# Gated linear mixer with five small experts: keys' level factors on VectorE, the norm's gains folded into the copies of the turned rows

## The chip, the cores and the metric

The kernel runs on 1 core of one Trainium2 chip. The metric is the device time of the whole program in microseconds (us), lower is better. Before the change the median of 3 runs is 1949.45 us (1948.65, 1949.45 and 1952.14).

## The reference

256 tokens of width 1024 go through a first block (three attention branches with gates and a feed-forward) and then a second block of two layers. The change lies in the mixer of the second block's first layer, a gated linear recurrence of 8 heads of width 128:

- from the rows h: forget gates f (a sigmoid, scaled between a lower bound and 1), queries q (silu), values v, output gates g (a sigmoid), keys k = 1 - f;
- for each head a running sum c of log f over the tokens; the output of token t is the sum over s up to t of (q_t exp(c_t - c_s) k_s) v_s;
- the output of each head is divided by its root mean square, multiplied by the vector `hg_norm_g_2` (128 gains, the same for each head) and by the gate g, and multiplied by `hg_w_out_2`.

Behind it follow a layer norm, a feed-forward of width 2816, a second layer with differential attention, and 8 experts of width 3584 for the chosen tokens.

## The kernel before

The program is written by hand for each engine, with semaphores. Every weight is read from HBM into a ring of three 2 MB slots (SP's queue, `load`), cut into pieces, and each piece is split into a high part (ScalarE, L1255) and a low part (VectorE, L1862); each product of rows and weights is then three matmuls (TensorE, L437 to L439). A slot is loaded again as soon as VectorE has split its last piece. VectorE's and ScalarE's programs are sequences in a fixed order: `pieces_done` and `piece_done` stand between the other work and take one piece each.

**The mixer's stage** (some 480 to 640 us of the profile). The recurrence is not run over tokens but in levels. For a block size b of 128, 64, 32, 16, 8, 4, 2, 1 (`LEVELS`, levels 0 to 7) tokens are taken in pairs of blocks; a query in the second block of a pair meets a key in the first, and the decay between them is split at the block's border into a factor of the query and one of the key. Level 8 is the diagonal, without factors. For each level:

- `level_differences` (VectorE, L2243; L2240 for level 0): the sums c minus c at the border, 128x2048;
- `level_exps` (ScalarE, L1540 and L1541): the two exponentials, 128x1024 each, the keys' and the queries';
- `level_queries` (VectorE, L2253): queries times factor into QS, 128x1024;
- `level_keys` (GpSimd, L2844): keys times factor into KS, 128x1024, with the other operands in the same form;
- `level` (TensorE, L885): 32 matmuls of 128x128 in fp32 (16 for level 0) of KS and QS into four PSUM banks; it waits for both factors;
- `level_place` (VectorE, L2263, levels 2 and up): four masked copies from PSUM into STT. Levels 0 and 1 are copied by ScalarE (`level_copy`, L1552, L1554).

The levels stand between the projections for g and v: TensorE does two pieces of a projection (24 matmuls of 512 columns) and then one level (`LEVEL_AT`). VectorE does two splits, the next level's differences, this level's four copies, the next level's queries. QS and KS exist once, so the queries and keys of a level wait for the matmuls of the level before (`T["level", i - 1]`).

The gate rows (GN, in the buffer BC) get tanh on ScalarE (L1561), times 0.5 plus 0.5 on VectorE (`gate_rows2`, L2270), and the norm's gains on GpSimd (`gain_gates`, L2852, four 128x512, with NG[:, 0] as a row spread over the partitions). GpSimd does `gain_gates("hg0")` behind level 3 and `gain_gates("hg1")` behind level 5. GpSimd also sets RM, STT, KS and QS and computes KK ahead of the levels (L2828 to L2835).

At the end VectorE multiplies the outputs by the root (L2312) and by GN (L2315), TensorE turns them (`columns("ho")`, L457), ScalarE copies the turned rows to XH (`column_halves`, L1273) and VectorE computes XL from PSUM and XH (`column_lows`, L1890), as operands for the product with `hg_w_out_2`. In the turned rows a partition is one of the 128 columns of a head. The vectors that are needed this way stand in VS, one row each, loaded by small DMAs of SP's queue at the start (`VECTORS`, L2943), turned once by TensorE into VT.

Of the kernel before, what the change touches and what calls it, by code (L numbers as in the profile page):

```python
# [53 lines left out]

V_MIX, V_MEM, V_FFN, V_LNG, V_LNB, V_QF, V_KF, V_QC, V_KC, V_LB = 0, 8, 16, 24, 56, 88, 89, 90, 91, 92

# [66 lines left out]
def build(nc, I, table, out):  # L123
    ctx = ExitStack()
    with ctx:
# [17 lines left out]
        BC = sb("BC", [128, 2, D])  # L143
        NG = sb("NG", [128, 2, 128])
        GM = sb("GM", [128, 2, 64])
# [63 lines left out]
        s_ed, s_ee, s_qs, s_ks, s_lv, s_stt, s_vv = (sem(n) for n in ("s_ed", "s_ee", "s_qs", "s_ks", "s_lv", "s_stt", "s_vv"))  # L209
        s_gth, s_gg, s_ggp, s_osq, s_od = (sem(n) for n in ("s_gth", "s_gg", "s_ggp", "s_osq", "s_od"))  # L210
        s_lam, s_lme, s_rx, s_ru, s_mix, s_dsq, s_doo = (sem(n) for n in ("s_lam", "s_lme", "s_rx", "s_ru", "s_mix", "s_dsq", "s_doo"))
# [125 lines left out]
        PM, PMT = ar(AR1, 2048, 2, 512), ar(AR1, 3072, 2, 512)  # L337
        VECTORS = [(V_FFN, "g_ffn", 8), (V_LNG, "ln_g_2", 32), (V_LNB, "ln_b_2", 32), (V_LB, "hg_lb_2", 24), (V_QC, "g_q_mem", 1), (V_KC, "g_k_mem", 1)]
        ONE = AR1[:, 17408:17536]
# [79 lines left out]
        def pe_program(e):  # L419
# [261 lines left out]
            room(7)  # L681
            pe.wait_ge(s_vec, 16 * 10)
            e.transpose(PS[7][:, 0:128], VS[:, 0:128], ident).then_inc(banks.put("vt", 7), 1)
# [553 lines left out]
        def act_program(e):  # L1237
# [25 lines left out]

            def column_halves(name, scale=None, tts=(0, 1), halves=(0, 1)):
                for tt in tts:
                    a.wait_ge(*T["xfree", name, tt])
                    for half in halves:
                        j = 2 * tt + half
                        a.wait_ge(*banks.full["cols", name, j])
                        ps = PS[banks_of[name][j]].rearrange("p (a n) -> p a n", a=4)  # L1270
                        x = XH[:, 4 * half:4 * half + 4, 128 * tt:128 * tt + 128]
                        if scale is None:
                            e.activation(x, ps, ACT.Copy).then_inc(s_colh, 1)  # L1273
                        else:
                            a.wait_ge(*banks.out["vt0" if scale == V_MEM else "vt"])
                            for k in range(4):
                                c = scale + 4 * half + k
                                t = e.activation(x[:, k, :], ps[:, k, :], ACT.Copy, scale=VT[:, c:c + 1])
                            t.then_inc(s_colh, 1)
# [311 lines left out]
            for tt in range(2):  # L1591
                for g in range(2):
# [3 lines left out]
                    e.activation(SQ2[:, tt, 512 * g:512 * g + 512], PS[2 * tt + g][:, :], ACT.Square).then_inc(s_osq, 1)  # L1596
            column_halves("ho")

# [252 lines left out]
        def dve_program(e):  # L1851
# [28 lines left out]

            def column_lows(name, scale=None, tts=(0, 1), halves=(0, 1)):
                for tt in tts:
                    for half in halves:
                        j = 2 * tt + half
                        v.wait_ge(s_colh, col_at(name, tt, half))
                        ps = PS[banks_of[name][j]].rearrange("p (a n) -> p a n", a=4)
                        xs = (slice(None), slice(4 * half, 4 * half + 4), slice(128 * tt, 128 * tt + 128))
                        h2, l2 = XH[xs], XL[xs]
                        if scale is None:
                            e.tensor_tensor(l2, ps, h2.bitcast(F32), ALU.subtract).then_inc(s_cols, 1)  # L1890
                        else:
                            for k in range(4):
                                c = scale + 4 * half + k
                                t = e.scalar_tensor_tensor(out=l2[:, k, :], in0=ps[:, k, :], scalar=VT[:, c:c + 1], in1=h2[:, k, :].bitcast(F32), op0=ALU.mult, op1=ALU.subtract)
                            t.then_inc(s_cols, 1)
# [26 lines left out]
            def unit_rows(n):  # L1922
                nh = HEADS[n]
                for tt in range(2):
# [10 lines left out]
                    if n in GAIN_ROW:  # L1935
                        v.wait_ge(s_bc, 16 * 8)
                        v.wait_ge(*banks.out["p", n, tt])
                        e.tensor_tensor(x, x, GM[:, GAIN_ROW[n], :].unsqueeze(1).to_broadcast([128, 8, 64]), ALU.mult).then_inc(s_gn, 1)
# [41 lines left out]
            def forget(stage):  # L1980
                if stage == 0:
                    v.wait_ge(*banks.full["fg", 0])
                    e.tensor_copy(NCT[0:8], PS[3][0:8, 0:256]).then_inc(banks.out["fg", 0][0], 1)
                    v.wait_ge(*banks.full["fg", 1])
                    v.wait_ge(s_bc, 16 * 8)
                    e.tensor_tensor(FZ, PS[3][:, 256:272].rearrange("p (a h) -> p a h", a=2), BFG[:, :].unsqueeze(1).to_broadcast([128, 2, 8]), ALU.add).then_inc(banks.out["fg", 1][0], 1)
# [78 lines left out]
            first_layer(ITEMS[2:4])  # L2065
            v.wait_ge(s_bc, 16 * 8)
            for i, w in enumerate((WFG, WRT)):
# [177 lines left out]
            def level_queries(i):  # L2245
# [7 lines left out]
                e.tensor_tensor(qsv[:, :, 1, :], qv[:, :, 1, :], ev[:, :, 1, :], ALU.mult).then_inc(s_qs, 1)  # L2253

            def level_place(i):

                for n in range(2):
                    for g in range(2):
                        b = 4 + (2 * n + g + 2) % 4
                        v.wait_ge(*banks.full["lv", i, n, g])  # L2260
                        v.wait_ge(s_set, 2)
                        m = LEVM[:, 128 * (i - 1):128 * i].unsqueeze(1).to_broadcast([128, 4, 128])
                        e.copy_predicated(STT[:, n, 4 * g:4 * g + 4, :], m, PS[b][:, :].rearrange("p (j n) -> p j n", j=4)).then_inc(banks.out["lv", i, n, g][0], 1)  # L2263
# [20 lines left out]
            pieces_done(4)  # L2284
            level_queries(0)
            for n in ("hg0", "hg1", "hv0", "hv1"):
                for q in range(4):
# [3 lines left out]
                    if (n, q) in LEVEL_AT:  # L2291
# [5 lines left out]
                        if i + 1 < 8:  # L2297
                            level_queries(i + 1)
            level_place(8)
            for tt in range(2):  # L2300
# [4 lines left out]
            v.wait_ge(s_ee, 8)  # L2305
            v.wait_ge(s_ggp, 4)
            for tt in range(2):
                for g in range(2):
# [6 lines left out]
                    e.tensor_tensor(ov, ov, GN[:, tt, 512 * g:512 * g + 512], ALU.mult).then_inc(s_od, 1)  # L2315
            column_lows("ho")
            norm_between(0, ("ho0", "ho1"), ((0, 1), (6, 7)), "F2")
# [22 lines left out]
            t_nl = v.step(e.tensor_scalar(NL, NL, -LAM_INIT, None, ALU.add))  # L2340
            t_ng = v.step(e.tensor_scalar(NG[:, 1, :], NG[:, 1, :], 1.0 - LAM_INIT, None, ALU.mult))

# [35 lines left out]
            def da_rows(g):  # L2378
                r = root(("da", g))
                for q in range(2):  # L2380
# [4 lines left out]
                    v.wait_ge(*t_ng)  # L2385
                    e.tensor_tensor(ov, ov, NG[:, 1, :].unsqueeze(1).to_broadcast([128, 4, 128]), ALU.mult).then_inc(s_doo, 1)

# [350 lines left out]
        def pool_program(e):  # L2738
# [44 lines left out]
            for tt in range(2):  # L2783
                inverse_root(("kc", tt))
            for dst, name, n in ((GM[:, 0, :], "g_q_moba", 64), (GM[:, 1, :], "g_k_moba", 64), (NG[:, 0, :], "hg_norm_g_2", 128),
                                 (NG[:, 1, :], "da_norm_g_2", 128), (LAMB[:, :], "da_lam_2", 256), (BFG[:, :], "b_forget", 8)):
                e.dma_start(dst, spread(I[name], n)).then_inc(s_bc, 16)
# [42 lines left out]
            e.memset(STT, 0.0).then_inc(s_set, 1)  # L2830
            t_ks = p.step(e.memset(KS, 0.0))
            p.wait_ge(s_sg, 8)
            e.tensor_scalar(KK, SG, -1.0, 1.0, ALU.mult, ALU.add).then_inc(s_kk, 1)
            p.wait_ge(*T["scan"])
            e.memset(QS, 0.0).then_inc(s_q0, 1)  # L2835
            p.wait_ge(*t_ks)
            p.wait_ge(s_kk, 1)

            def level_keys(i):
                ev, kv, ksv = (flat(x).rearrange("p (y x b) -> p y x b", x=2, b=LEVELS[i]) for x in (EE, KK, KS))  # L2840
                p.wait_ge(s_ee, i + 1)
                if i:
                    p.wait_ge(*T["level", i - 1])
                e.tensor_tensor(ksv[:, :, 0, :], kv[:, :, 0, :], ev[:, :, 0, :], ALU.mult).then_inc(s_ks, 1)  # L2844

            def gain_gates(n):
                c = int(n[2])
                p.wait_ge(s_bc, 16 * 8)
                for tt in range(2):
                    g4 = GN[:, tt, 512 * c:512 * c + 512].rearrange("p (h d) -> p h d", h=4)  # L2850
                    p.wait_ge(s_gg, 2 * c + tt + 1)
                    e.tensor_tensor(g4, g4, NG[:, 0, :].unsqueeze(1).to_broadcast([128, 4, 128]), ALU.mult).then_inc(s_ggp, 1)  # L2852

            level_keys(0)
            for i in range(1, 8):
                level_keys(i)
                if i == 3:
                    gain_gates("hg0")
                if i == 5:
                    gain_gates("hg1")  # L2860
            for tt in range(2):
# [259 lines left out]
```

## Time and profile before

| | us |
|---|---|
| median of 3 runs | 1949.45 |
| the profiled execution | 1949.79 |
| its span, first to last instruction | 1948.0 |
| TensorE busy | 1846.0 (95%) |
| VectorE busy | 1487.8 (76%) |
| ScalarE busy | 1219.4 (63%) |
| GpSimd busy | 166.6 (9%) |

The granted clock of TensorE is 0.98 of full over the span. The busy shares are means over stages with different limits. For this change only the stage with the levels counts, and there the duration of a single VectorE instruction beside GpSimd's, and the starts of the level's matmuls, say more than a share.

### The profile page before, as it was taken

The numbers are of one execution on the slowest core, as the hardware profiler recorded it, in microseconds if no ns is written. First come the engines' busy times: TensorE is split into PE (matmuls) and PEld (weight loads), VectorE is DVE, ScalarE is ACT, GpSimd is POOL, SyncE is SP. The second block draws the span as 40 slices with busy tenths as digits, with TensorE's granted clock in tenths as the row PEclk, the third lists the DMA queues.
The fourth block names the chain that finished last, engine by engine and source line by source line (L and its number), as shares of the span: only waits on it lengthen the run. The fifth ranks groups of instructions, "written<-read, shape, count | busy, mean of one in ns | idle before, by whom it ended". The sixth has DMA issues, their size and how long they took to land.

```text
span 1948.0 us, 22339 instructions
## 1 busy us (share of the span) xinstructions
PE 1846.0 (95%) x9128; PEld 1527.8 (78%) x9128; DVE 1487.8 (76%) x1424; ACT 1219.4 (63%) x1267; POOL 166.6 (9%) x128
## 2 busy tenths in 40 slices
PE   7999999999998899988979999999999999999997
PEld 6888878888987688877757887877888787788875
DVE  5645566444689754467678989999988999998897
ACT  6555546343653444335536778888777888877784
POOL 2501100000233310023120000000000000000000
PEclk9999999999999999989988999999999999999999
DMA  8434445445432465435246999999999999999994
GB/s 290 172 130 136 151 175 187 174 172 195 146 114 87 152 229 182 151 136 181 95 175 224 379 353 399 409 413 409 404 370 365 400 409 413 409 405 371 358 410 177
DMA packets 154813, 511.61 MB, mean 263 GB/s; under 512 B 4447, under 2 KB 8913, under 8 KB 140369
## 3 DMA queue, kind: packets, MB, share of 16 engines
q1 hardware_dynamic: 152672, 504.53, 68.3%
q0 software_dynamic: 1424, 4.59, 0.8%
q8 instruction: 74, 1.21, 0.3%
q10 hardware_dynamic: 608, 0.99, 0.1%
q14 instruction: 35, 0.28, 0.0%
HBM read 509.05 MB, written 1.05 MB: 262 GB/s over the span
## 4 chain that ended last, share of the span: by engine, by line
PE 68%; DVE 18%; DMA 7%; ACT 4%; issue 2%; POOL 0%; ACTq 0%; SPq 0%; DVEq 0%; POOLq 0%
PE PS L437 19%; PE PS L439 18%; PE PS L438 18%; DVE WLB L1862 6%; DMA ring<-in_moe_w_down 6%; DVE WLX L1862 5%; PE PS L1104 1%; PE PS L1105 1%; ACT WHX L1255 1%; ACT WHB L1255 1%; PE PS L885 1%; PE PS L1035 1%; PE PS L1037 1%; DVE AR L2253 1%; PE PS L582 1%
## 5 line engine op out<-in xcount | busy, mean ns | idle before, releaser
L1862 DVE TENSOR_TENSOR WLB<-ring,WHB 128x2048 fp32r<-128x2048 f32 (+1 forms) x344 | 645.9, 1894 | 118.6 <-ACT WHB L1255 118.1
L1255 ACT ACTIVATE WHB<-ring 128x2048 fp32r<-128x2048 f32 (+1 forms) x344 | 532.6, 1561 | 317.9 <-PE PS L439 283.9
L1862 DVE TENSOR_TENSOR WLX<-ring,WHX 128x2048 fp32r<-128x2048 f32 (+1 forms) x216 | 469.0, 2192 | 54.2 <-ACT WHX L1255 54.0
L1255 ACT ACTIVATE WHX<-ring 128x2048 fp32r<-128x2048 f32 (+1 forms) x216 | 393.4, 1838 | 160.1 <-PE PS L439 124.3
L437 PE MATMUL PS<-WHB,XH 128*128 128x512 f32 (+1 forms) x640 | 259.2, 405 | 14.8 <-DVE XL L1911 6.8
L439 PE MATMUL PS<-WHB,XL 128*128 128x512 f32 (+1 forms) x640 | 251.2, 392 | 0.0
L438 PE MATMUL PS<-WLB,XH 128*128 128x512 f32 (+1 forms) x640 | 250.8, 392 | 0.0
L437 PEld LDWEIGHTS PS<-WHB,XH 128*128 128x128 f32 x640 | 123.0, 192 | 43.5 <-issue 11.7
L2743 POOL TENSOR_TENSOR SM<-SM,MH 128x8 f32<-128x8 f32 (+3 forms) x28 | 38.2, 1368 | 1352.8 <-DVE SM L1875 1352.8
L439 PEld LDWEIGHTS PS<-WHB,XL 128*128 128x128 f32 x640 | 122.6, 192 | 26.5
L438 PEld LDWEIGHTS PS<-WLB,XH 128*128 128x128 f32 x640 | 123.1, 192 | 23.4
L1058 PE MATMUL PS<-WHB,EH 128*128 128x512 f32 x280 | 113.0, 404 | 4.2 <-DVE WLB L1862 3.3
L1058 PE MATMUL PS<-WHX,EH 128*128 128x512 f32 x280 | 113.7, 406 | 3.5 <-DVE WLX L1862 2.5
L1059 PE MATMUL PS<-WLX,EH 128*128 128x512 f32 x280 | 109.6, 391 | 0.0
L1059 PE MATMUL PS<-WLB,EH 128*128 128x512 f32 x280 | 109.5, 391 | 0.0
L437 PE MATMUL PS<-WHX,XH 128*128 128x512 f32 (+1 forms) x240 | 92.2, 384 | 4.7 <-DVE WLX L1862 4.7
L439 PE MATMUL PS<-WHX,XL 128*128 128x512 f32 (+1 forms) x240 | 91.0, 379 | 0.0
L438 PE MATMUL PS<-WLX,XH 128*128 128x512 f32 (+1 forms) x240 | 90.8, 378 | 0.0
L437 PE MATMUL PS<-WHB,HTH 128*128 128x512 f32 x184 | 72.3, 393 | 0.0
L439 PE MATMUL PS<-WHB,HTL 128*128 128x512 f32 x184 | 71.7, 390 | 0.0
L438 PE MATMUL PS<-WLB,HTH 128*128 128x512 f32 x184 | 71.6, 389 | 0.0
L1058 PEld LDWEIGHTS PS<-WHB,EH 128*128 128x128 f32 x280 | 52.6, 188 | 22.5 <-DVE WLB L1862 12.3
(416 smaller groups left out, 3441.4 us busy)
## 6 DMA issues: line engine op xcount, KB each, us to landing
ring<-in_moe_w_gate SPq DMA_DIRECT2D x56, 2048.0 KB, 11.0
ring<-in_moe_w_up SPq DMA_DIRECT2D x56, 2048.0 KB, 11.3
ring<-in_moe_w_down SPq DMA_DIRECT2D x56, 2048.0 KB, 11.8
ring<-in_w_in SPq DMA_DIRECT2D x13, 2048.0 KB, 8.1
ring<-in_hg_w_in SPq DMA_DIRECT2D x8, 2048.0 KB, 8.5
ring<-in_da_w_in SPq DMA_DIRECT2D x6, 2048.0 KB, 8.0
ring<-in_w_gate SPq DMA_DIRECT2D x5, 2048.0 KB, 7.8
ring<-in_w_up SPq DMA_DIRECT2D x5, 2048.0 KB, 7.8
```

The source lines that it names most:

```text
L437: e.matmul(o, xh, wh, start=start, stop=False)
L438: e.matmul(o, xh, wl, start=False, stop=False)
L439: return e.matmul(o, xl, wh, start=False, stop=stop)
L582: t = e.matmul(PS[4 + q][:, dv * h:dv * h + dv], PTBUF[a][h % 2][:, 128 * j:128 * j + 128], VR[VK[a]][:, k, dv * h:dv * h + dv], start=(k ...
L885: t = e.matmul(PS[b][:, 128 * j:128 * j + 128], a_k[:, h, 128 * s_t:128 * s_t + 128], a_q[:, h, 128 * t_t:128 * t_t + 128], start=True, st ...
L1035: t = e.matmul(PS[b][:, at_:at_ + 64], src[:, tt, 128 * d:128 * d + 128], PO[:, tt, 0:64], start=(tt == 0), stop=(tt == 1))
L1037: t = e.matmul(PS[b][:, 128 * j:128 * j + CAP], src[:, tt, 128 * d:128 * d + 128], PO[:, tt, :], start=(tt == 0), stop=(tt == 1))
L1058: e.matmul(PS[b][:, :], EH[:, kt, :], wh, start=(kt == 0), stop=False)
L1059: t = e.matmul(PS[b][:, :], EH[:, kt, :], wl, start=False, stop=(kt == 7))
L1255: e.activation(hi, src, ACT.Copy).then_inc(s_hi, 1)
L1862: e.tensor_tensor(lo, src, hi.bitcast(F32), ALU.subtract).then_inc(s_lo, 1)
L2743: e.tensor_tensor(RR[name], RV[name], MH[:, 0:RR[name].shape[1]], ALU.pow).then_inc(s_rs, 1)
```

## The change

`level_keys` moves from GpSimd's program to VectorE's, behind `level_queries` of the same level. `gain_gates` goes away; the gains come in as a per-partition scale in ScalarE's copy of the turned rows and in VectorE's low part of them. For this `hg_norm_g_2` is loaded by SP's queue as row 116 of VS (a DMA more) instead of being spread into NG by GpSimd's queue (a DMA less), and NG is half as large. VectorE waits for s_gg where it waited for s_ggp.

```diff
-V_MIX, ..., V_LB = 0, 8, 16, 24, 56, 88, 89, 90, 91, 92
+V_MIX, ..., V_LB, V_HN = 0, 8, 16, 24, 56, 88, 89, 90, 91, 92, 116
-        NG = sb("NG", [128, 2, 128])
+        NG = sb("NG", [128, 128])
-        VECTORS = [..., (V_LB, "hg_lb_2", 24), (V_QC, "g_q_mem", 1), ...]
+        VECTORS = [..., (V_LB, "hg_lb_2", 24), (V_HN, "hg_norm_g_2", 1), (V_QC, "g_q_mem", 1), ...]
-            pe.wait_ge(s_vec, 16 * 10)
+            pe.wait_ge(s_vec, 16 * 11)
 # ScalarE, column_halves(..., one=None)
+                        if one is not None:
+                            e.activation(x, ps, ACT.Copy, scale=VT[:, one:one + 1]).then_inc(s_colh, 1)
-            column_halves("ho")
+            column_halves("ho", one=V_HN)
 # VectorE, column_lows(..., one=None)
+                        if one is not None:
+                            e.scalar_tensor_tensor(out=l2, in0=ps, scalar=VT[:, one:one + 1], in1=h2.bitcast(F32), op0=ALU.mult, op1=ALU.subtract).then_inc(s_cols, 1)
-                        v.wait_ge(s_bc, 16 * 8)
+                        v.wait_ge(s_bc, 16 * 7)
 # VectorE
+            def level_keys(i):
+                ev, kv, ksv = (flat(x).rearrange("p (y x b) -> p y x b", x=2, b=LEVELS[i]) for x in (EE, KK, KS))
+                v.wait_ge(s_ee, i + 1)
+                v.wait_ge(s_set, 3)
+                v.wait_ge(s_kk, 1)
+                if i:
+                    v.wait_ge(*T["level", i - 1])
+                e.tensor_tensor(ksv[:, :, 0, :], kv[:, :, 0, :], ev[:, :, 0, :], ALU.mult).then_inc(s_ks, 1)
             level_queries(0)
+            level_keys(0)
...
                             level_queries(i + 1)
+                            level_keys(i + 1)
-            v.wait_ge(s_ggp, 4)
+            v.wait_ge(s_gg, 4)
-            column_lows("ho")
+            column_lows("ho", one=V_HN)
 # GpSimd
-            t_ks = p.step(e.memset(KS, 0.0))
+            e.memset(KS, 0.0).then_inc(s_set, 1)
...
-            def level_keys(i): ...
-            def gain_gates(n):
-                c = int(n[2])
-                p.wait_ge(s_bc, 16 * 8)
-                for tt in range(2):
-                    g4 = GN[:, tt, 512 * c:512 * c + 512].rearrange("p (h d) -> p h d", h=4)
-                    p.wait_ge(s_gg, 2 * c + tt + 1)
-                    e.tensor_tensor(g4, g4, NG[:, 0, :].unsqueeze(1).to_broadcast([128, 4, 128]), ALU.mult).then_inc(s_ggp, 1)
-            level_keys(0)
-            for i in range(1, 8):
-                level_keys(i)
-                if i == 3:
-                    gain_gates("hg0")
-                if i == 5:
-                    gain_gates("hg1")
```

## Rows read from the trace of the kernel before

**Rows 1.** The page, part 2: the DMA engines' busy tenths in 40 slices of the span

```profile
DMA  8434445445432465435246999999999999999994
```

**Rows 2.** The chain that ended last, inside the levels (start us, us, what)

```profile
579.99 2.20 DVE AR L2243
582.19 2.54 DVE AR L2263 x4
...
587.74 1.13 DVE WLB L1862
588.87 0.67 DVE BC L2270 x2
```

**Rows 3.** Windows from level to level: length, busy PE, PEld, DVE, ACT, POOL; clock; DMA

```profile
575.60:587.80 12.20, 9.36 (x57) 8.02 (x57) 12.20 (x9) 4.17 (x5) 5.65 (x3) 1.00 0.00 0
587.80:598.60 10.80, 10.80 (x56) 9.69 (x57) 10.80 (x11) 3.69 (x4) 3.58 (x2) 0.84 0.55 196
```

**Rows 4.** Timeline of VectorE (DVE) in the levels

```profile
561.41 1.23 DVE L2253 TENSOR_TENSOR AR<-AR 128x1024 f32<-128x1024 f32 x1 [3.46 <-ACT AR L1541]
562.55 3.41 DVE L1862 TENSOR_TENSOR WLB<-ring,WHB 128x1024 fp32r<-128x1024 f32 x1
...
572.40 3.17 DVE L2253 TENSOR_TENSOR AR<-AR 128x1024 f32<-128x1024 f32 x1
575.49 4.50 DVE L1862 TENSOR_TENSOR WLB<-ring,WHB 128x1024 fp32r<-128x1024 f32 x2
...
618.15 3.84 DVE L2253 TENSOR_TENSOR AR<-AR 128x1024 f32<-128x1024 f32 x1
```

**Rows 5.** Timeline of GpSimd (POOL) in the levels

```profile
561.45 3.42 POOL L2844 TENSOR_TENSOR AR<-AR 128x1024 f32<-128x1024 f32 x1 [7.93 <-ACT AR L1541]
572.09 2.40 POOL L2844 TENSOR_TENSOR AR<-AR 128x1024 f32<-128x1024 f32 x1 [7.22 <-ACT AR L1541]
574.45 4.46 POOL L2852 TENSOR_TENSOR BC<-BC,NG 128x512 f32<-128x512 f32 x2
...
618.03 2.88 POOL L2844 TENSOR_TENSOR AR<-AR 128x1024 f32<-128x1024 f32 x1 [7.85 <-ACT AR L1541]
```

**Rows 6.** TensorE's level matmuls: timeline for levels 1 to 4, chain for 7, 8

```profile
553.62 5.44 PE L885 MATMUL PS<-AR 128*128 128x128 f32 x32 [2.02 <-issue]
564.98 3.81 PE L885 MATMUL PS<-AR 128*128 128x128 f32 x32 [0.40 <-issue]
575.62 3.84 PE L885 MATMUL PS<-AR 128*128 128x128 f32 x32 [1.33 <-DVE AR L2253]
587.79 5.46 PE L885 MATMUL PS<-AR 128*128 128x128 f32 x32 [2.82 <-DVE AR L2253]
...
622.31 7.15 PE PS L885 x64
```

**Rows 7.** Timeline of ScalarE: the exponentials of levels 1 and 2

```profile
549.01 1.04 ACT L1541 ACTIVATE AR<-AR 128x1024 f32<-128x1024 f32 x1
...
559.38 1.05 ACT L1540 ACTIVATE AR<-AR 128x1024 f32<-128x1024 f32 x1
```

**Rows 8.** Single lines: copies and subtractions with and without a pointer scale (min/median/max ns)

```profile
L1353 ACT ACTIVATE AR<-PS,VT x4: 669/674/681, 33.5 to 68.0; 128x512 f32<-128x512 f32 x4
...
L1273 ACT ACTIVATE XH<-PS x16: 592/597/600, 275.8 to 990.8; 128x512 fp32r<-128x512 f32 x16
...
L1932 DVE SCALAR_TENSOR_TENSOR AR<-PS,SM x2: 739/740/741, 30.1 to 30.8; 128x512 f32<-128x512 f32 x2
...
L1890 DVE TENSOR_TENSOR XL<-PS,XH x16: 681/684/692, 277.9 to 991.5; 128x512 fp32r<-128x512 f32 x16
```

**Rows 9.** Timeline of the start: a small DMA of SP's queue, ScalarE's third split

```profile
6.77 0.25 SPq L2944 DMA_DIRECT2D VS<-in_g_k_mem  x1
...
23.64 1.06 ACT L1255 ACTIVATE WHB<-ring 128x1024 fp32r<-128x1024 f32 x1 [0.42 <-PE PS L439]
```

**Rows 10.** Waits of SP's queue over the span: total us, times, longest

```profile
SPq L2933 <- DVE WLB L1862: 1154.4, 132, 32.8
```

More of the change, by code:

```diff
@@ L53 @@
 C_END = 2112
-V_MIX, V_MEM, V_FFN, V_LNG, V_LNB, V_QF, V_KF, V_QC, V_KC, V_LB = 0, 8, 16, 24, 56, 88, 89, 90, 91, 92
+V_MIX, V_MEM, V_FFN, V_LNG, V_LNB, V_QF, V_KF, V_QC, V_KC, V_LB, V_HN = 0, 8, 16, 24, 56, 88, 89, 90, 91, 92, 116
 def constant_table():
@@ L209, in build @@
         s_ed, s_ee, s_qs, s_ks, s_lv, s_stt, s_vv = (sem(n) for n in ("s_ed", "s_ee", "s_qs", "s_ks", "s_lv", "s_stt", "s_vv"))
-        s_gth, s_gg, s_ggp, s_osq, s_od = (sem(n) for n in ("s_gth", "s_gg", "s_ggp", "s_osq", "s_od"))
+        s_gth, s_gg, s_osq, s_od = (sem(n) for n in ("s_gth", "s_gg", "s_osq", "s_od"))
         s_lam, s_lme, s_rx, s_ru, s_mix, s_dsq, s_doo = (sem(n) for n in ("s_lam", "s_lme", "s_rx", "s_ru", "s_mix", "s_dsq", "s_doo"))
@@ L337, in build @@
         PM, PMT = ar(AR1, 2048, 2, 512), ar(AR1, 3072, 2, 512)
-        VECTORS = [(V_FFN, "g_ffn", 8), (V_LNG, "ln_g_2", 32), (V_LNB, "ln_b_2", 32), (V_LB, "hg_lb_2", 24), (V_QC, "g_q_mem", 1), (V_KC, "g_k_mem", 1)]
+        VECTORS = [(V_FFN, "g_ffn", 8), (V_LNG, "ln_g_2", 32), (V_LNB, "ln_b_2", 32), (V_LB, "hg_lb_2", 24), (V_HN, "hg_norm_g_2", 1), (V_QC, "g_q_mem", 1), (V_KC, "g_k_mem", 1)]
         ONE = AR1[:, 17408:17536]
@@ L1262, in piece_done, with column_halves @@
                 split_to(done[0] + 3)
-            def column_halves(name, scale=None, tts=(0, 1), halves=(0, 1)):
+            def column_halves(name, scale=None, tts=(0, 1), halves=(0, 1), one=None):
                 for tt in tts:
@@ L1271, in column_halves @@
                         x = XH[:, 4 * half:4 * half + 4, 128 * tt:128 * tt + 128]
-                        if scale is None:
+                        if one is not None:
+                            e.activation(x, ps, ACT.Copy, scale=VT[:, one:one + 1]).then_inc(s_colh, 1)
+                        elif scale is None:
                             e.activation(x, ps, ACT.Copy).then_inc(s_colh, 1)
@@ L1879, in root, with column_lows @@
                 return RR[name]
-            def column_lows(name, scale=None, tts=(0, 1), halves=(0, 1)):
+            def column_lows(name, scale=None, tts=(0, 1), halves=(0, 1), one=None):
                 for tt in tts:
@@ L1888, in column_lows @@
                         h2, l2 = XH[xs], XL[xs]
-                        if scale is None:
+                        if one is not None:
+                            e.scalar_tensor_tensor(out=l2, in0=ps, scalar=VT[:, one:one + 1], in1=h2.bitcast(F32), op0=ALU.mult, op1=ALU.subtract).then_inc(s_cols, 1)
+                        elif scale is None:
                             e.tensor_tensor(l2, ps, h2.bitcast(F32), ALU.subtract).then_inc(s_cols, 1)
@@ L1984, in forget @@
                     v.wait_ge(*banks.full["fg", 1])
-                    v.wait_ge(s_bc, 16 * 8)
+                    v.wait_ge(s_bc, 16 * 7)
                     e.tensor_tensor(FZ, PS[3][:, 256:272].rearrange("p (a h) -> p a h", a=2), BFG[:, :].unsqueeze(1).to_broadcast([128, 2, 8]), ALU.add).then_inc(banks.out["fg", 1][0], 1)
@@ L2065, in dve_program @@
             first_layer(ITEMS[2:4])
-            v.wait_ge(s_bc, 16 * 8)
+            v.wait_ge(s_bc, 16 * 7)
             for i, w in enumerate((WFG, WRT)):
@@ L2340, in dve_program @@
             t_nl = v.step(e.tensor_scalar(NL, NL, -LAM_INIT, None, ALU.add))
-            t_ng = v.step(e.tensor_scalar(NG[:, 1, :], NG[:, 1, :], 1.0 - LAM_INIT, None, ALU.mult))
+            t_ng = v.step(e.tensor_scalar(NG[:, :], NG[:, :], 1.0 - LAM_INIT, None, ALU.mult))
             def rope_rows(n, i):
@@ L2385, in da_rows @@
                     v.wait_ge(*t_ng)
-                    e.tensor_tensor(ov, ov, NG[:, 1, :].unsqueeze(1).to_broadcast([128, 4, 128]), ALU.mult).then_inc(s_doo, 1)
+                    e.tensor_tensor(ov, ov, NG[:, :].unsqueeze(1).to_broadcast([128, 4, 128]), ALU.mult).then_inc(s_doo, 1)
             def da_mix(h):
@@ L2784, in pool_program @@
                 inverse_root(("kc", tt))
-            for dst, name, n in ((GM[:, 0, :], "g_q_moba", 64), (GM[:, 1, :], "g_k_moba", 64), (NG[:, 0, :], "hg_norm_g_2", 128),
-                                 (NG[:, 1, :], "da_norm_g_2", 128), (LAMB[:, :], "da_lam_2", 256), (BFG[:, :], "b_forget", 8)):
+            for dst, name, n in ((GM[:, 0, :], "g_q_moba", 64), (GM[:, 1, :], "g_k_moba", 64),
+                                 (NG[:, :], "da_norm_g_2", 128), (LAMB[:, :], "da_lam_2", 256), (BFG[:, :], "b_forget", 8)):
                 e.dma_start(dst, spread(I[name], n)).then_inc(s_bc, 16)
@@ L2835, in pool_program @@
             e.memset(QS, 0.0).then_inc(s_q0, 1)
[L2836 to L2844, printed above, removed]
-            def gain_gates(n):
-                c = int(n[2])
-                p.wait_ge(s_bc, 16 * 8)
-                for tt in range(2):
-                    g4 = GN[:, tt, 512 * c:512 * c + 512].rearrange("p (h d) -> p h d", h=4)
-                    p.wait_ge(s_gg, 2 * c + tt + 1)
-                    e.tensor_tensor(g4, g4, NG[:, 0, :].unsqueeze(1).to_broadcast([128, 4, 128]), ALU.mult).then_inc(s_ggp, 1)
-            level_keys(0)
-            for i in range(1, 8):
-                level_keys(i)
-                if i == 3:
-                    gain_gates("hg0")
-                if i == 5:
-                    gain_gates("hg1")
             for tt in range(2):
```

## The prediction

> **What bounds the kernel now.** I began with the slices of the page. In the second half, where the experts are, the DMA engines are busy nine tenths and more; in the mixer's stage, slices 11 to 13, they are busy four tenths or less [rows 1]. So the stage of this change is not bound by loads. The chain of waits says by what: from 575 to 611 us it runs nearly all through VectorE, in the order splits, differences (2.20 us), four masked copies (2.54), queries, splits (1.13 each where nothing disturbs them), now and then the two gate rows (0.67) [rows 2]. The windows from one level's matmuls to the next agree: VectorE is busy 12.20 us of 12.20 and 10.80 of 10.80, TensorE has gaps in the first of them [rows 3].
>
> Why a level takes 12.2 or 10.8 us shows only in single instructions. The queries' product of level 2 starts at 561.41 and the next VectorE instruction at 562.55: 1.14 us for it. The split behind it takes 3.41 us and not 1.13, the queries of level 3 take 3.17, those of level 7 3.84, and two splits at 575.49 take 4.50 [rows 4]. Beside each stands a GpSimd instruction, and each such VectorE instruction ends about one undisturbed length after GpSimd's end [rows 4, 5]: keys of level 2 end at 564.87, the split at 565.96; keys of level 3 end at 574.49, the queries at 575.57; keys of level 7 end at 620.91, the queries at 621.99. With the four gain products (2.23 us each, two of them at 574.45) it is one split per product, 2.25 instead of 1.13. So VectorE does not run slower beside GpSimd, it stands still while GpSimd's instruction runs. The Trainium skill, SBUF — State Buffer, section "SBUF: two separate sides", calls the shared port pair an exclusive lock held for a whole instruction; by that rule, the trace agrees.
>
> **The change part by part.**
>
> *Keys on VectorE.* Eight products of 128x1024 are added. Price: the same form for the queries, 1.15 us with its step to the next. Its ends are 1.08 (what is left of the queries behind GpSimd's end) and 3.84, the longest row of that form [rows 4]; I take 1.15, because small blocks give 1.08 once GpSimd is out of the way. Behind each keys' product VectorE has the two splits queued, and TensorE's level waits for it: both are counted below. The waits it adds (s_kk, s_set) are for GpSimd work that ends before the levels, and ScalarE's exponentials are the queries' own wait; these cost nothing.
>
> *GpSimd gone from the stage.* Removed are about 2.0 us of standstill per level in seven levels and 1.12 us for each of four gain products.
>
> *A VectorE period without GpSimd:* 2 x 1.13 + 2.20 + 2.54 + 2 x 1.15 = 9.3 us, and with a gate pair 9.97. ScalarE must fit in: both exponentials take 2.05 us behind the differences and are covered by the 2.54 us of copies.
>
> *TensorE's period.* Level 2 to level 3 is 575.62 - 564.98 less 1.33 idle = 9.3 us at full clock; level 4 to 5 is 10.8 us at a granted clock of 0.84, since the level takes 5.46 instead of 3.84 us [rows 3, 6]. The level took the long form behind idle gaps of 2.02 and 2.82 us, and the short one behind 0.40 and 1.33. The new gaps are under 1 us, so I take full clock (2.4 GHz); each level that falls to the lower clock costs 1.6 us. TensorE and VectorE are then tied at 9.3.
>
> *The new starts.* The exponentials of level 1 end at 550.05 as before (ScalarE was loading a table while the differences ended, so 1.1 us of delay there is covered) [rows 7]. Queries and keys end at 552.35: level 1 starts at 552.4, gap 0.9, was 553.62. VectorE: two splits and differences to 556.8; exponentials to 558.9 (they wait for level 1's copies too, which ended 0.3 us behind that level before [rows 6, 7], so at 556.5); queries and keys to 561.2. TensorE is ready at 552.4 + 9.25. Level 2 starts at 561.7, was 564.98. VectorE's next period holds a gate pair: 561.2 + 9.97 gives level 3 at 571.2, was 575.62. Then level 4 at 580.5 (587.79), level 5 with the second gate pair at 590.5, level 6 at 599.8 and level 7 at 609.1, was 622.31. From there to the end of level 8 nothing but 64 matmuls in 7.15 us counts, as before. Gain 13.2 us.
>
> *The norm's gains in the copies.* ScalarE's copy with a pointer scale takes 0.674 us against 0.597, VectorE's scalar_tensor_tensor 0.740 against 0.684 [rows 8]: at most 4 x 0.077 + 4 x 0.056 = 0.5 us, at least 0. They run beside TensorE's last transposes and have a product of 5 us and more before their later halves are used, so I take 0.1. By the Trainium skill, ScalarE: Activation LUTs, section "What ACT_TABLE_LOAD costs", each pointer operand adds about 93 ns; by that the first term would be an estimated 0.37 instead of 0.31, which the same cover hides.
>
> *Loads at the start.* SP's queue issues one more small DMA, 0.3 us with its step, ahead of the second and third weight load; ScalarE's splits of that load have 0.42 us in hand before TensorE lets the next go on [rows 9]. Zero, at most 0.3. GpSimd issues one DMA fewer, with a long idle behind it: zero. NG's smaller size moves later buffers by 512 bytes: zero either way, I know of no row that prices it.
>
> *Down to the end.* Later loads are not started by a clock: SP's queue waits 132 times for VectorE's splits, 1154 us in all [rows 10]. So the loads move with the work, those of the experts too, and the gain stays.
>
> Sum: -13.2 + 0.1 = -13.1. The profiled execution took 1949.79 us (span 1948.0 and 1.8 around it) and should take 1936.7; it lies 0.34 above the median 1949.45, so the median becomes **1936.4 us**.
>
> **The rivals.**
>
> 1. *The clock stays low.* TensorE has no slack, so each level that runs at the lower clock adds 1.6 us. It fell in levels 1, 4 and 6; three of them again give 1941.3. For it: the levels' short fp32 matmuls come often. Against: two levels behind small gaps ran at full clock [rows 6].
> 2. *Slower: the long queries are VectorE's own.* The queries took 3.1 us and more just in the levels with blocks of 16 and less. If small blocks were the cause, keys of the same form would cost as much on the engine that is busy without a gap. It decides if less than 1.15 us per period comes back. Price: five periods by 1.15 to 3.1 us, +5.7 to +15.5, so 1955 to 1965. Against: splits, which have no blocks, are lengthened the same way, and all ends follow GpSimd's ends [rows 4, 5]. The Trainium skill, Perfetto Trace Analysis, section "Optimizing Scalar/DVE Operations", advises to offload a saturated VectorE, even to GpSimd, which speaks against this change, though it adds that the shared port may make that useless.
> 3. *The gain is taken back.* The expert stage has its DMA engines full [rows 1]. If its loads ran on their own clock, a start 13 us earlier would be waited off: no change, 1949.5. Against it are SP's waits [rows 10].
> 4. *It doesn't do what it says:* something of GpSimd would have to remain among the levels. The diff leaves only the roots behind them; I give it no chance of its own. A partial gain for a wait that I overlooked (near 5 us, 1944) gets one.
>
> **How the numbers follow.** Forecast 0.70, rival 1 0.17, partial gain 0.04, rival 3 0.05, rival 2 0.04. A measurement of this kernel can tell about 0.2%, 3.9 us, from no change. Faster: 0.91, same 0.05, slower 0.04. The range takes in the forecast with the run's own scatter of about 1 us and a TensorE period shorter by 0.1 (1934.4) and up to rival 1 with a microsecond on top (1942.4); left out are the last three.
>
> **What would show it right or wrong.** After: L2253's and the keys' line on VectorE at 1.23 us each in all eight levels; all splits of the stage at 1.2; level starts 9.3 us apart, level 7 near 609; GpSimd idle between 530 and 620; the level's 32 matmuls at 3.8 us. A split or query still above 2 us would overthrow the standstill, 5.4 us levels mean rival 1, a level 7 near 609 with an unchanged end rival 3.

## The result and the profile after

The changed kernel takes 1935.24 us in the median of 5 runs (1932.16 to 1937.5), the kernel before 1949.45 us in its 5 (1946.14 to 1952.14): ratio 0.9925, 95% interval 0.9907 to 0.9942, 14.2 us faster. Forecast were 1936.4 us and 13.1 us. The profiled execution took 1933.71 us with a span of 1931.9 us, 16.1 us less than that of before; 13.1 of these lie between the matmuls of level 0 and of level 7.

The timeline of TensorE, levels 1 to 7 (levels 7 and 8 are one row), against [rows 6]. The granted clock is 1.00 from level 0 to level 7. The bracket at the end of a line is the time that the engine stood idle just before it, here called the gap.

```profile
551.39 3.81 PE L885 MATMUL PS<-AR 128*128 128x128 f32 x32 [0.94 <-issue]
560.54 3.73 PE L885 MATMUL PS<-AR 128*128 128x128 f32 x32
570.21 3.81 PE L885 MATMUL PS<-AR 128*128 128x128 f32 x32 [0.42 <-issue]
579.45 3.81 PE L885 MATMUL PS<-AR 128*128 128x128 f32 x32
589.36 3.81 PE L885 MATMUL PS<-AR 128*128 128x128 f32 x32 [0.59 <-issue]
598.61 3.81 PE L885 MATMUL PS<-AR 128*128 128x128 f32 x32
607.85 7.38 PE L885 MATMUL PS<-AR 128*128 128x128 f32 x64
```

Levels are 9.2 us apart, or 9.7 and 9.9 where VectorE also has two gate rows to do (a gate pair), and every level takes 3.7 or 3.8 us. Gaps are left ahead of levels 1, 3 and 5.

VectorE's timeline around levels 3 and 4 (L2257 queries, L2266 keys, L1864 splits, L2283 gate rows, L2247 differences, L2276 masked copies), against [rows 4]:

```profile
567.76 1.22 DVE L2257 TENSOR_TENSOR AR<-AR 128x1024 f32<-128x1024 f32 x1
568.89 1.22 DVE L2266 TENSOR_TENSOR AR<-AR 128x1024 f32<-128x1024 f32 x1
570.02 2.36 DVE L1864 TENSOR_TENSOR WLB<-ring,WHB 128x1024 fp32r<-128x1024 f32 x2
572.29 2.29 DVE L2247 TENSOR_TENSOR AR<-AR 128x2048 f32<-128x2048 f32 x1
574.50 2.62 DVE L2276 COPY_PREDICATED AR<-LEVM,PS 128x512 f32<-128x512 uint16 x4
```

The keys' line alone (min/median/max ns over all block sizes), and the copies with the gains, the answers to [rows 8]:

```profile
L2266 DVE TENSOR_TENSOR AR<-AR x8: 1205/1218/1239, 541.1 to 606.5; 128x1024 f32<-128x1024 f32 x8
```

```profile
L1273 ACT ACTIVATE XH<-PS,VT x4: 687/688/688, 624.9 to 628.9; 128x512 fp32r<-128x512 f32 x4
```

```profile
L1892 DVE SCALAR_TENSOR_TENSOR XL<-PS,VT,XH x4: 743/744/752, 627.6 to 629.7; 128x512 fp32r<-128x512 f32 x4
```

The eight keys' products cost 1.2 us each, the smallest blocks as much as the largest. (On GpSimd the same products took 2.34 to 2.40 us in levels 3 to 5 of the kernel before, but 2.82 and 2.88 us in levels 6 and 7, with blocks of 2 and 1. Whether the blocks are the reason was not tested.) Windows from level 2 to 3 and 3 to 4 (columns as in [rows 3]):

```profile
560.60:570.20 9.60, 9.19 (x57) 7.86 (x56) 9.60 (x12) 4.99 (x6) 0.00 (x0) 1.00 0.62 218
570.20:579.50 9.30, 9.29 (x57) 8.07 (x57) 9.30 (x10) 4.24 (x5) 0.00 (x0) 1.00 0.01 3
```

GpSimd is idle, VectorE busy without a gap, and TensorE too where no gate pair stands: the tie that was forecast.

### The profile page after: what moved, and what is told of

Read it like the earlier page. It is cut to its first block, busy times and chain, and to the rows that moved or that the text cites. A ratio compares the mean times of both kernels' runs of the same rounds, so it can differ in the third digit from the quotient of the medians.

```text
span 1931.9 us, 22326 instructions
## 1 busy us (share of the span) xinstructions
PE 1838.0 (95%) x9128; PEld 1520.4 (79%) x9128; DVE 1476.1 (76%) x1432; ACT 1219.4 (63%) x1267; POOL 135.0 (7%) x115
## 3 DMA queue, kind: packets, MB, share of 16 engines
q8 instruction: 74, 1.21, 0.2%
## 4 chain that ended last, share of the span: by engine, by line
PE 69%; DVE 16%; DMA 7%; ACT 4%; issue 2%; POOL 0%; ACTq 0%; SPq 0%; DVEq 0%; POOLq 0%
PE PS L437 19%; PE PS L439 19%; PE PS L438 19%; DMA ring<-in_moe_w_down 6%; DVE WLX L1864 5%; DVE WLB L1864 5%; PE PS L885 2%; PE PS L1104 1%; PE PS L1105 1%; ACT WHX L1255 1%; ACT WHB L1255 1%; PE PS L1035 1%; PE PS L1037 1%; PE PS L582 1%; DMA ring<-in_moe_w_gate 1%
## 5 line engine op out<-in xcount | busy, mean ns | idle before, releaser
L1864 DVE TENSOR_TENSOR WLB<-ring,WHB 128x2048 fp32r<-128x2048 f32 (+1 forms) x344 | 635.3, 1863 | 119.3 <-ACT WHB L1255 118.8
L1864 DVE TENSOR_TENSOR WLX<-ring,WHX 128x2048 fp32r<-128x2048 f32 (+1 forms) x216 | 468.5, 2189 | 53.8 <-ACT WHX L1255 53.5
L1058 PEld LDWEIGHTS PS<-WHX,EH 128*128 128x128 f32 x280 | 52.6, 188 | 22.0 <-DVE WLX L1864 11.6
## 6 DMA issues: line engine op xcount, KB each, us to landing
ring<-in_moe_w_down SPq DMA_DIRECT2D x56, 2048.0 KB, 12.3
```

Source lines behind the costliest of these rows:

```text
L1058: e.matmul(PS[b][:, :], EH[:, kt, :], wh, start=(kt == 0), stop=False)
L1864: e.tensor_tensor(lo, src, hi.bitcast(F32), ALU.subtract).then_inc(s_lo, 1)
```

## The experiments

The theory to be tested: VectorE stood still while a GpSimd instruction read SBUF. The rivals: the long instructions belonged to small blocks or to waits for the keys; only one half of the change counted; some of the gain lies outside the levels. The way from level 0 to level 7 is the measure within one profile, since two executions of one kernel can reach level 0 more than a microsecond apart (the table below).

### Keys alone

The kernel before with this (the edit, shortened):

```diff
+                            level_keys(i + 1)      # VectorE, behind level_queries; GpSimd's level_keys removed
-            for i in range(1, 8): level_keys(i) ...
+            gain_gates("hg0")                      # GpSimd, as before, waits for the gate rows alone
+            gain_gates("hg1")
```

> The kernel before with the keys' products on VectorE and the four gain products still on GpSimd (they now wait for the gate rows alone, so they fall beside the splits behind them). Theory (VectorE stands still for the time a GpSimd instruction reads SBUF, and VectorE and TensorE are tied once that is gone): the keys' share of the gain, each gain product still costs 1.12 us of VectorE in a period that VectorE bounds, 4.5 in all: 1939.7 us against 1935.2, level 7 some 8.7 us earlier than before. Rival (long instructions belong to small blocks): the keys cost VectorE 1.15 to 3.1 us each for nothing: 1955 to 1965. Rival (the gain came from the gain products): 1949 to 1951.

Measured: 1936.34 us (5 runs), ratio to before 0.9941 (0.9927 to 0.9955). Level 0 at 541.58, level 7 at 608.88: 67.3 us, where the kernel before has 78.0 and the changed one 64.9. So the keys give 10.7 us of the 13.1, not 8.7; the rivals (no gain, or slower) are out. The 2 us that the expectation was short show in the two pairs of gain products. GpSimd's gain products, and VectorE beside the first pair:

```profile
560.64 3.54 POOL L2853 TENSOR_TENSOR BC<-BC,NG 128x512 f32<-128x512 f32 x2 [33.13 <-DVE BC L2279]
581.90 6.04 POOL L2853 TENSOR_TENSOR BC<-BC,NG 128x512 f32<-128x512 f32 x2 [17.72 <-DVE BC L2279]
```

```profile
560.74 2.29 DVE L1862 TENSOR_TENSOR WLB<-ring,WHB 128x1024 fp32r<-128x1024 f32 x1
562.95 3.37 DVE L2243 TENSOR_TENSOR AR<-AR 128x2048 f32<-128x2048 f32 x1
...
582.03 1.25 DVE L1862 TENSOR_TENSOR WLB<-ring,WHB 128x1024 fp32r<-128x1024 f32 x1
583.17 2.32 DVE L2243 TENSOR_TENSOR AR<-AR 128x2048 f32<-128x2048 f32 x1
585.37 2.68 DVE L2272 COPY_PREDICATED AR<-LEVM,PS 128x512 f32<-128x512 uint16 x4
```

The first pair cost VectorE 1.1 us twice, as priced. The second cost it nothing: this time it was GpSimd that stood still. It needed 6.04 us for two products, of which the quicker took 1.31, and was through at 587.94, in the time of the masked copies. One of the two engines pays, and not always the same one.

### Gains alone

The changed kernel with `level_keys` back on GpSimd.

> The kernel before with the gains in the copies of the turned rows and the keys' products still on GpSimd. Theory: VectorE loses 1.12 us less beside each of four products, and the level behind a shorter gap runs at full clock: level 7 at 617.5 instead of 622.3 (counted from the start of the kernel before), 1944.6 us. With keys_only the two gains should add up to that of the whole change, 8.7 + 4.8 = 13.5. Rival (the copies with a pointer scale lie on the path): 0.5 us of it is lost. Rival (the gain products were covered): 1949.5.

Measured: 1944.52 us (11 runs, 1939.21 to 1948.12), ratio to before 0.9977 (0.9968 to 0.9986). Level 0 at 543.79, level 7 at 617.48: 73.7 us, 4.3 less than before (expected 4.8). Level 4 stands behind a gap of 0.70 us instead of 2.82 and takes 3.84 us instead of 5.46, as expected:

```profile
585.31 3.84 PE L885 MATMUL PS<-AR 128*128 128x128 f32 x32 [0.70 <-DVE AR L2257]
```

The faster levels are not where the gain comes from. From level 3 to 4 and from 5 to 6, where the gain products ran, the way is 2.12 and 2.04 us shorter than before; from 4 to 5 and from 6 to 7, where levels 4 and 6 are now at full clock, it is 0.04 and 0.10 us shorter, since VectorE needed the time anyway. The two halves give 10.7 + 4.3 = 15.0 us where the whole gives 13.1. With the keys still on GpSimd both pairs of gain products cost some 2.1 us; with the keys on VectorE only the first did, and 13.1 - 10.7 = 2.4 us were left to gain (2.2 there, 0.2 ahead of level 1).

### A reader of SBUF beside the levels

The changed kernel, and on GpSimd behind the fill of QS:

```diff
+            p.wait_ge(s_tab, 16)
+            for i in range(8):
+                p.wait_ge(s_ee, i + 1)
+                p.wait_ge(*p.step(e.tensor_tensor(ring4[:, 3328:4096], CT[:, 0:768], CT[:, 128:896], ALU.mult)))
```

> The changed kernel, and GpSimd does a product of its own beside each level: 128x768, reads two stretches of the constants, writes a stretch of SBUF that nobody reads; nobody waits for it. It starts at the same signal as the keys did. Theory (VectorE stands still while GpSimd reads): each takes some 1.8 us and VectorE's period grows by that, 12 to 13 us over the levels: 1947 us, and in the timeline queries, keys or splits of about 3 us. Rival (what cost time before was a wait for the keys or the shape of the products, not the neighbour): 1935.2 us, all VectorE instructions at 1.2.

Measured: 1948.67 us (10 runs), ratio to before 1.0002 (0.9993 to 1.0012). Products that nobody waits for take nearly the whole gain back: level 0 at 543.59, level 7 at 620.71, 77.1 us, 12.3 more than the changed kernel. Seven of the eight lie in that way. Each period grows by 1.5 to 1.7 us, as VectorE's instructions beside the reader do; the one from level 1 to 2 grows by 2.6. There level 1 ran behind a gap of 2.56 us at a granted clock of 0.70, took 5.32 us, and ScalarE's exponentials stood behind its copies. So some 11 us are the standstill and 1 us is the clock. Level 3, GpSimd first, then VectorE:

```profile
572.60 1.86 POOL L2854 TENSOR_TENSOR ring<-CT 128x768 f32<-128x768 f32 x1 [8.41 <-ACT AR L1543]
```

```profile
572.85 2.70 DVE L2257 TENSOR_TENSOR AR<-AR 128x1024 f32<-128x1024 f32 x1
575.47 1.21 DVE L2266 TENSOR_TENSOR AR<-AR 128x1024 f32<-128x1024 f32 x1
```

GpSimd ends at 574.46, the queries at 575.55, 1.09 us later, which is what was left of the queries behind GpSimd in the kernel before (1.08). The keys behind them, of the same blocks and with nothing beside them, take 1.21. The shape is not the cause, nor is a wait for a result: the neighbour is.

### A writer beside the levels

The same with `e.memset(ring4[:, 3328:4096], 1.0)` three times in place of the product.

> The changed kernel, and GpSimd fills the same stretch of SBUF three times beside each level (128x768, some 0.7 us each, 2.1 us together); nobody waits for it. Theory (the standstill needs a GpSimd instruction that reads SBUF; the fill of QS beside two splits in the kernel before left them at 1.18 each): 1935.2 us, VectorE unchanged. The Trainium skill, SBUF - State Buffer, section SBUF: two separate sides, says that a VectorE operation with two SBUF inputs is held up only by a GpSimd operation that reads SBUF; it gives the same. Rival (any GpSimd instruction stops VectorE): 2.1 us per level, 1949 us.

Measured: 1936.69 us (4 runs), ratio to before 0.9935 (0.992 to 0.9951); level 0 at 543.37, level 7 at 608.24: 64.9 us, the same as without it.

```profile
568.13 1.22 DVE L2257 TENSOR_TENSOR AR<-AR 128x1024 f32<-128x1024 f32 x1
569.26 1.22 DVE L2266 TENSOR_TENSOR AR<-AR 128x1024 f32<-128x1024 f32 x1
```

```profile
567.87 2.35 POOL L2854 MEMSET ring<- 128x768 f32 x3 [7.24 <-ACT AR L1543]
```

2.35 us of fills beside both products lengthen neither. The Trainium skill, SBUF — State Buffer, section "SBUF: two separate sides", says so too: two SBUF inputs on VectorE meet only a GpSimd operation that reads SBUF. The trace agrees, for a fill against such products.

### A reader beside the masked copies

The changed kernel with the reader's product five times, started by `p.wait_ge(s_ed, i)` for i from 4 to 8, when the differences are done.

> The changed kernel, and GpSimd does the product of read_beside (128x768, 1.85 us) in levels 2 to 6, started when the differences are done, so beside the four masked copies, which read one operand from SBUF and one from PSUM. Theory (only VectorE instructions with two SBUF operands stand still): VectorE unchanged at 2.6 us for four copies, 1935.2 us, level 0 to 7 in 64.9. Rival (any VectorE instruction stands still beside a GpSimd read): 5 x 1.5 = 7.5 us, 1942.7.

Measured: 1936.71 us (4 runs), ratio to before 0.9946 (0.9931 to 0.9962); level 0 at 541.42, level 7 at 606.61: 65.2 us. From level 1 to level 7 it is 56.6 us against 56.5; the other 0.2 us are a longer gap ahead of level 1, which also shows in two kernels without this product.

```profile
573.40 1.88 POOL L2854 TENSOR_TENSOR ring<-CT 128x768 f32<-128x768 f32 x1 [7.45 <-DVE AR L2247]
```

```profile
573.17 2.64 DVE L2276 COPY_PREDICATED AR<-LEVM,PS 128x512 f32<-128x512 uint16 x4
```

The same GpSimd product that costs 1.5 us beside the queries costs nothing beside copies that take one operand from SBUF and the other from PSUM. The copies are also another kind of instruction than the products; whether the operand's place or the kind decides was not separated.

### Both kernels once more

> The kernel before, unchanged. Between the profiled executions before and after 16.1 us of span went, 13.1 of them from level 0 to level 7. If the other 3 are scatter of one execution (TensorE's clock falling at other moments), level 0 starts between 541.5 and 544.2 here and the way from level 0 to level 7 is 78.0 us again. If they belong to the change, level 0 starts at 544.15 and the product behind the mixer is slow again.

> The changed kernel, unchanged. Scatter: level 0 starts up to 1.5 us off 542.99, the way from level 0 to 7 is 64.9 us within 0.2. Change: all as in the first profile.

Measured, one execution each, 1946.16 and 1936.3 us:

| | level 0 starts | level 0 to 7 | level 7 to the end of the span |
|---|---|---|---|
| before, first profile | 544.15 | 78.0 | 1325.9 |
| before, second | 542.66 | 76.6 | 1325.1 |
| after, first | 542.99 | 64.9 | 1324.1 |
| after, second | 544.29 | 64.9 | 1325.4 |

Start and tail (the last column) scatter by 1 to 2 us in both kernels and in no fixed direction, and over the ten profiles of this document the tail takes 1322.8 to 1328.0 us. So nothing shows that the 3 us of the 16.1 that lie outside the levels belong to the change; with two profiles of each kernel a few tenths can't be excluded. The product behind the mixer, which the expectation names, was slow again (3.83 and 3.66 us from its first matmul to its tenth), but in the second profile of the changed kernel nearly as much (2.85 and 3.52 us). The levels of the changed kernel repeat to the tenth. Those of the kernel before don't: in the second profile level 1 ran at full clock behind the same gap.

```profile
552.12 3.81 PE L885 MATMUL PS<-AR 128*128 128x128 f32 x32 [2.01 <-issue]
```

That was 3.81 us against 5.44 in [rows 6], and the way was 1.4 us shorter. The expectation of 78.0 us again missed by that.

### The gate rows on ScalarE

The changed kernel, with VectorE's `gate_rows2` taken out and put on ScalarE, four pieces behind the tanh (the edit, shortened):

```diff
+                    e.activation(g, g, ACT.Copy, bias=0.5, scale=0.5).then_inc(s_gg, 1)
```

> The changed kernel with the gate rows' times 0.5 plus 0.5 on ScalarE in place of VectorE. Theory (VectorE and TensorE are tied at 9.3 us, only the two periods with a gate pair are bounded by VectorE): TensorE's gaps of 0.42 and 0.59 us ahead of levels 3 and 5 go, level 0 to level 7 takes 63.9 us instead of 64.9, the time 1934.2 us, which timing can't tell from 1935.2. Rival (VectorE bounds all periods): 1.3 us and more. Rival (ScalarE's exponentials are late now): a gap of 0.6 to 1.2 us comes in place, no gain.

Measured: 1933.56 us (5 runs, 1929.64 to 1934.9), ratio to before 0.9931 (0.9917 to 0.9944). Level 0 at 541.30, level 7 at 605.01: 63.7 us, 1.2 less than the changed kernel. The gaps ahead of levels 3 and 5 are gone:

```profile
568.17 3.73 PE L885 MATMUL PS<-AR 128*128 128x128 f32 x32
577.29 3.81 PE L885 MATMUL PS<-AR 128*128 128x128 f32 x32
586.53 3.81 PE L885 MATMUL PS<-AR 128*128 128x128 f32 x32
```

From level 1 on all periods are 9.1 to 9.2 us. The way came out near the 63.9 expected, but this does not show that TensorE alone bounds the levels: from level 2 on VectorE has no gap either. Level 0 to 1 took 0.2 us longer than in the changed kernel, and from level 1 to 7 it is 55.1 us against 56.5. These 1.4 us are what two gate pairs take on VectorE (0.67 each), more than the two gaps (1.0) that the theory gave; 1.3 us was the rival's number. The late exponentials are out; which of the two engines sets the period is open. As a version it beats both kernels in the trace; the timing can tell it from before, not from the changed kernel.

## Why the prediction was right

- **The standstill.** The step on which all rested, that VectorE's long instructions were GpSimd's doing and not their own, is shown by the reader (1948.67 us, nearly all back) against the writer and the reader beside the copies (1936.7 both). All splits, queries and keys of the stage are at 1.2 us in the changed kernel.
- **Price of the keys.** Taken 1.15 us with the step to the next instruction, measured 1.13 (568.89 to 570.02).
- **The starts.** Counted from level 0, which began 1.16 us earlier in this execution, the forecast starts of levels 1 to 7 are 551.2, 560.5, 570.0, 579.3, 589.3, 598.6 and 607.9; measured are 551.39, 560.54, 570.21, 579.45, 589.36, 598.61 and 607.85. None is off by more than 0.2 us. (The forecast of 13.2 us took the old level 7 from the chain, 622.31. In the timeline it starts at 622.14; by that the forecast is 13.0 and the measured gain 13.1.)
- **The clock.** All seven levels ran at full clock, also in the second profile; the rival with three slow levels didn't come. But the ground given for it, that the size of the gap decides, is too simple. Behind gaps of 2.01 and 2.02 us level 1 took 3.81 us in one execution of the kernel before and 5.44 in the other. With the keys alone level 3 took 3.81 us behind a gap of 2.59, and with the reader level 3 was slow behind 2.08 and level 5 fast behind 2.14:

```profile
571.21 3.81 PE L885 MATMUL PS<-AR 128*128 128x128 f32 x32 [2.59 <-issue]
```

```profile
576.78 5.44 PE L885 MATMUL PS<-AR 128*128 128x128 f32 x32 [2.08 <-issue]
598.94 3.81 PE L885 MATMUL PS<-AR 128*128 128x128 f32 x32 [2.14 <-issue]
```

  Shown is only that no level behind a gap of 1.6 us or less was slow in any profile. The 1.6 us per slow level that rival 1 was priced with were never put to a test in a kernel where TensorE has no slack.
- **The gains in the copies.** 0.688 and 0.744 us against 0.597 and 0.684. From TensorE's last transposes to its first matmul with the turned rows it is 0.77 us in both kernels (642.00 to 642.77 and 627.78 to 628.55), and to the first that reads the low part 1.77 us in both (to 643.77 and 629.55); nothing of the 0.1 us shows.
- **The start.** ScalarE got the second weight load at 21.55 instead of 21.20 us in the first profiles, and at 21.17 instead of 21.12 in the second. Level 0 came 1.16 us earlier than before in the first and 1.63 later in the second. If SP's extra DMA costs anything, it is lost in this scatter; zero was taken.
- **Pass-through.** From level 7 to the end it takes 1324 to 1325 us against 1325 to 1326. Nothing of the 13 us is taken back there.
- **The size.** 14.2 us in the medians against 13.1; the 13.1 us in the levels are the forecast 13.2, and the rest is within the scatter of start and tail.
- **The slower rival** fell by its own condition: far more than 1.15 us per period came back. The advice named beside it, from the Trainium skill, Perfetto Trace Analysis, section "Optimizing Scalar/DVE Operations", to offload a saturated VectorE even to GpSimd, would have kept the standstill that this change removed; its reservation about the shared port held.

## What to carry to other kernels

Where VectorE is saturated, look at the duration of single instructions beside GpSimd's: if the same form takes 1.2 us at one place and 3.2 at another and ends one plain length behind a GpSimd instruction, work on GpSimd isn't free, and 1.2 us on VectorE is cheaper than 2.4 us beside it. In this kernel a GpSimd product was free beside masked copies on VectorE that take an operand from PSUM, and fills were free beside products, so such places are the first to try for GpSimd's work.

## What was not expected

- GpSimd can be the one that stands still. For the length of one VectorE instruction this already showed in the kernel before: the keys of level 2 started 0.04 us behind the queries and took 3.42 us, those of level 3 took 2.40 [rows 4, 5]. With VectorE's instructions back to back it lasted longer: 6.04 us for two products, of which the quicker took 1.31, while VectorE lost nothing; the first pair of the same kernel cost VectorE 2.2 us. What decides which engine gets through was not settled. The pairs start 0.10 and 0.13 us ahead of a split of the same form.
- The same gap of 2.0 us ahead of level 1 left TensorE at full clock in one execution and at the lower one in another (3.81 and 5.44 us for the level, a granted clock of 1.00 and 0.69 over it).
